# Moving the mLSTM scores, exponents and norms of a hybrid decoder layer in among its token projections

## The chip, the cores and the metric

The kernel runs on one core of one Trainium2 chip. The metric is the device time of one call in microseconds; the time before is the median of three runs. The engines are TensorE (PE, with PEld for its weight loads), VectorE (DVE), ScalarE (ACT), GpSimd (POOL) and SyncE (SP), which issues nearly all DMAs. Each engine works through its own list of instructions in order; the engines meet only at semaphores.

## The reference, cut to what matters

One decoder layer on 256 prompt tokens and 8 sequences of 4 sample tokens (288 columns in all), model width 1024: RMS norm, one input projection of 2824 columns, three mixers side by side, one output projection, and then a mixture of 32 experts (top 4 of 32, two matrices each), all in float32. The three mixers read disjoint columns of the projection: S5 (a diagonal complex recurrence, width 256, gelu, and a gated linear unit), RG-LRU (width 256), and mLSTM (4 heads of 128). The mLSTM part is what is changed most:

```python
mt = jnp.maximum(inter, jnp.max(dmat, axis=-1))
s = einsum('bhtd,bhsd->bhts', qc, kc) * exp(dmat - mt[..., None])     # decay matrix times scores
sc = exp(inter - mt)
num = einsum('bhts,bhsd->bhtd', s, vc) + sc[..., None] * einsum('bhtk,bhkv->bhtv', qc, cm)
den = sum(s, axis=-1) + sc * einsum('bhtk,bhk->bht', qc, nv)
h = num / maximum(abs(den), exp(-mt))[..., None]
c_new = decay[..., None, None] * cm + einsum('bhs,bhsk,bhsv->bhkv', ws, kc, vc)
h = h * rsqrt(mean(h * h) + EPS) * norm_g;   y = h * sigmoid(o)
```

The experts' weights are 32 x 12 MB, 403 MB in all; everything else that is read is about 23 MB.

## The kernel before, in words

The program is one block with one hand-ordered list for each engine. Its stages:

1. **Norm and input projection (0 to about 138 us).** x is normalised and turned into `hT` (channels x tokens). The projection's weights come in six chunks w_in0 to w_in5 through three slots of a ring. PE makes `channels` (a weight block stationary, 288 tokens moving, 16 matmul records each) for u, xr, gr, q and k, and `tokens` (tokens stationary, 256 weight columns moving) for v and o (`va`, `vb`, `oa`, `ob`, and `v2`, `o2` for the sample tokens).
2. **Gates and S5, in the same stretch.** DVE makes the mLSTM gate rows (`gsm`: a logarithm by a polynomial of eight steps, then scans), and says `m_rows` and `gate_rows`. ACT takes the exponentials of those rows and goes on to copy q2, q3, k0, k1 out of PSUM, in that order. POOL builds the S5 rotation table. Then S5 runs in eight pieces j: PE `s5_in(j)` fills two banks `bu{j}r` and `bu{j}i`, DVE `s5_scan(j)` rotates and scans them, POOL turns the result back (`s5_turned`), PE `s5_out(j)` adds it into `ys0` or `ys1`. RG-LRU work stands on DVE between the scans.
3. **mLSTM (about 138 to 190 us).** After the last token projection: gate rows turned (`rows`), the row maxima spread (`mb{h}`), scores (`st{h}`), on DVE the exponents' arguments and two multiplications, k turned (`kt`), memory products (`cp`), numerators (`nu`), on DVE the denominators and norms, on POOL k times its weights, v times its weights, and the decay of the state `c0` (L658).
4. **S5 gelu and gate.** DVE L1299 and L1300, then PE `glu`, ACT sigmoid, DVE `rg_used`.
5. **Output projection, residual, second norm, router (194 to 244 us)**, with the new sample state `c0` made on DVE by adding `cu` (L1313) and written out.
6. **Experts (from 244 us).** 16 pairs of experts of 12 steps each, 192 steps of 2 MB. Eight slots (`step_slot`: six in the ring, two in `ring_b`). SP may load step i once step i - 8 is done on PE. The eight first steps are loaded during stages 3 to 5 as the ring's slots come free.

PSUM has eight banks of 512 columns. The function `_place` gives each named fill a bank by its position in a list, and a number on that bank; `await_bank` lets PE start fill n of a bank only when fill n - 1 has been drained:

```python
def _place(names, banks):
    for i, name in enumerate(names):
        b = banks[i % len(banks)]
        FILLS[name] = (b, _fills_of[b])
        _fills_of[b] += 1
```

## Time and profile before

| | us |
|---|---|
| median of 3 runs (lowest, highest) | 1187.11 (1184.13, 1191.29) |
| the profiled execution, its time | 1186.5 |
| its span (first to last instruction) | 1184.8 |
| PE busy | 1110.9 (94%) |
| DVE busy | 364.8 (31%) |
| ACT busy | 163.4 (14%) |
| POOL busy | 137.9 (12%) |
| DMA over the span | 430.14 MB, mean 363 GB/s |

Busy shares are means over stages with different limits; the stages are told apart below by time from the span's start. In a timeline row the first number is the start, the second the busy time, then engine, line, operation, out<-in, shape and count; what stands in brackets is the idle time before it and who ended it. Matmuls in float32 leave two records each.

### The profile page before, as it was taken

Reading aid. Unit: us, or ns where it says so; the run is one execution under the profiler, and the core shown is the slowest. Engines: PE = TensorE matmul, PEld = TensorE weight load, DVE = VectorE, ACT = ScalarE, POOL = GpSimd, SP = SyncE. Lnnn points to the kernel's source line nnn. Section 1 sums busy time; section 2 is a strip of 40 time slices with the busy share of each in tenths; the row PEclk is TensorE's granted clock in tenths of the full one; section 3 lists DMA queues with packets and bytes.
Section 4 is the critical chain, followed back from the end, with each engine's and each line's share of the span. In section 5 each row is a group of like instructions: output and inputs, shape, how many; then the busy total and the mean of one; then the engine's idle time right before and its main releaser. Section 6 shows DMA issues by size and latency. Waiting matters only on the chain.

```text
span 1184.8 us, 12935 instructions
## 1 busy us (share of the span) xinstructions
PE 1110.9 (94%) x5051; PEld 463.6 (39%) x5051; DVE 364.8 (31%) x693; ACT 163.4 (14%) x304; POOL 137.9 (12%) x249
## 2 busy tenths in 40 slices
PE   6999767999999999999999999999999999999985
PEld 5766553443343334333433343333333332333221
DVE  5999985332121212121212122211312130203022
ACT  3312142211011001010101020101000100010002
POOL 7848753000000000000000000000000000000000
PEclk9989977999999999999999999999999999999998
DMA  8422343869999999999999999999999999999993
GB/s 228 157 92 71 130 177 142 320 266 392 427 426 422 427 428 426 427 429 428 426 429 429 427 428 429 428 426 429 429 427 428 429 428 427 429 429 426 428 428 150
DMA packets 79174, 430.14 MB, mean 363 GB/s; under 512 B 10730, under 2 KB 21202, under 8 KB 30242
## 3 DMA queue, kind: packets, MB, share of 16 engines
q1 hardware_dynamic: 78708, 428.47, 87.3%
q0 software_dynamic: 384, 1.18, 0.4%
q8 instruction: 22, 0.36, 0.1%
q14 instruction: 14, 0.11, 0.0%
q10 hardware_dynamic: 46, 0.01, 0.0%
HBM read 425.98 MB, written 3.67 MB: 363 GB/s over the span
## 4 chain that ended last, share of the span: by engine, by line
PE 67%; DVE 15%; DMA 12%; SPq 3%; ACT 1%; issue 1%; DVEq 0%; ACTq 0%
PE psum L1959 32%; PE psum L1972 15%; PE psum L1924 9%; DMA ring_a<-in_exp_w_dram 6%; DMA ring_b<-in_exp_w_dram 6%; PE psum L1934 4%; SPq L368 2%; PE psum L1983 1%; PE psum L1814 1%; PE psum L1943 1%; PE psum L1556 1%; DVE ring_a L1155 1%; DVE gsm L976 1%; DVE ring_a L1151 1%; DVE rgb L1299 1%
## 5 line engine op out<-in xcount | busy, mean ns | idle before, releaser
L1959 PE MATMUL psum<-ring_a,xg 128*64 128x512 f32 x1536 | 343.4, 596 | 7.6 <-DMA ring_a<-in_exp_w_dram 7.6
L1959 PEld LDWEIGHTS psum<-ring_a,xg 128*64 128x64 f32 x1536 | 105.0, 137 | 227.9 <-issue 210.1
L1972 PE MATMUL psum<-ring_a,aT 128*64 128x512 f32 x768 | 173.2, 597 | 8.8 <-DMA ring_a<-in_exp_w_dram 6.1
L1428 DVE TENSOR_TENSOR x<-x,psum 128x512 f32<-128x512 f32 x64 | 44.0, 688 | 364.6 <-PE psum L1934 364.6
L1959 PE MATMUL psum<-ring_b,xg 128*64 128x512 f32 x512 | 114.8, 595 | 0.2 <-DMA ring_b<-in_exp_w_dram 0.2
L1459 DVE TENSOR_SCALAR acts<-psum 128x512 f32<-128x512 f32 x32 | 22.0, 688 | 286.3 <-PE psum L1959 286.3
L1924 PE MATMUL psum<-S,xn 128*128 128x256 f32 (+1 forms) x384 | 109.0, 412 | 0.5 <-DVE S L1416 0.5
L1972 PEld LDWEIGHTS psum<-ring_a,aT 128*64 128x64 f32 x768 | 52.6, 136 | 110.6 <-issue 97.4
L1924 PEld LDWEIGHTS psum<-S,xn 128*128 128x128 f32 (+1 forms) x384 | 62.1, 187 | 53.6 <-issue 49.3
L1959 PEld LDWEIGHTS psum<-ring_b,xg 128*64 128x64 f32 x512 | 35.3, 137 | 73.6 <-issue 69.6
L884 ACT ACTIVATE acts<-acts 128x512 f32<-128x512 f32 x32 | 20.0, 626 | 316.4 <-DVE acts L1459 316.4
L1934 PE MATMUL psum<-yb,sgt 128*128 128x512 f32 x128 | 63.2, 617 | 0.0
L1556 PE MATMUL psum<-hT,ring_a 128*128 128x288 f32 x224 | 60.6, 433 | 1.9 <-DVE hT L994 1.4
L1972 PE MATMUL psum<-ring_b,aT 128*64 128x512 f32 x256 | 56.3, 592 | 1.4 <-DMA ring_b<-in_exp_w_dram 1.4
L877 ACT ACTIVATE xg<-psum 128x512 f32<-128x512 f32 x32 | 19.1, 598 | 276.7 <-PE psum L1924 276.7
L1556 PEld LDWEIGHTS psum<-hT,ring_a 128*128 128x128 f32 x224 | 45.4, 205 | 16.2 <-issue 3.2
L1432 DVE TENSOR_TENSOR x<-x,psum 32x256 f32<-32x256 f32 x64 | 26.5, 415 | 53.9 <-PE psum L1937 52.4
L1934 PEld LDWEIGHTS psum<-yb,sgt 128*128 128x128 f32 x128 | 21.8, 189 | 40.9 <-issue 40.9
L1972 PEld LDWEIGHTS psum<-ring_b,aT 128*64 128x64 f32 x256 | 18.7, 137 | 37.8 <-issue 37.3
L1565 PE MATMUL psum<-ring_a,hT 128*128 128x256 f32 x128 | 29.2, 384 | 2.1 <-DVE t_dve L1150 1.9
L1814 PE MATMUL psum<-ring_a,hT 128*128 128x512 f32 x64 | 30.5, 629 | 0.4 <-PE psum L1825 0.4
L909 ACT ACTIVATE yb<-psum 128x512 f32<-128x512 f32 x16 | 9.6, 597 | 140.2 <-PE psum L1972 140.2
(434 smaller groups left out, 825.8 us busy)
## 6 DMA issues: line engine op xcount, KB each, us to landing
ring_a<-in_exp_w_dram SPq DMA_DIRECT2D x144, 2048.0 KB, 25.9
ring_b<-in_exp_w_dram SPq DMA_DIRECT2D x47, 2048.0 KB, 27.4
ring_a<-in_w_in_dram SPq DMA_DIRECT2D x5, 2048.0 KB, 8.8
ring_a<-in_w_out_dram SPq DMA_DIRECT2D x2, 2048.0 KB, 10.1
ring_a<-in_state_ml_c_dram SPq DMA_DIRECT2D x4, 512.0 KB, 7.4
out_dram<-ring_a SPq DMA_DIRECT2D x4, 512.0 KB, 5.1
ring_b<-in_exp_w_dram SPq DMA_DIRECT2D x2, 1024.0 KB, 28.7
xn<-in_x_prompt_dram SPq DMA_DIRECT2D x2, 512.0 KB, 4.6
```

The costliest lines, as they stand in the source:

```text
L368: sp.dma_start(place, src).then_inc(slot_filled(il)[0], 16)
L884: A(sg1[:, x, :], gact[:, x, :], ACT.Sigmoid, scale=1.702).then_inc(sem("sig_ready"), 1)
L1428: TT(dst, dst, psum[0:n, banks[c], :], ALU.add).then_inc(sem("combine_added"), 1)
L1432: TT(dst, dst, psum[n * w:n * w + n, banks[c], 0:256], ALU.add).then_inc(sem("combine_added"), 1)
L1459: TSC(gact[:, x, :], psum[:, x, :], 7.0, None, ALU.min).then_inc(sem("g_clipped"), 1)
L1556: m = M(bank(name)[:, 0:T], w[:, k, col:col + 128], hT[:, k, :], start=(k == 0), stop=(k == KD - 1))
L1565: m = M(bank(name)[:, 0:256], hT[:, k, t0:t0 + n], w[:, k, col:col + 256], start=(k == 0), stop=(k == KD - 1))
L1814: m = M(bank(name)[0:n, :], hT[:, k, t0:t0 + n], slot_view(2 + c, 512)[:, k, :], start=(k == 0), stop=(k == KD - 1))
L1924: m = M(psum[:, 6 + c // 2 % 2, 256 * (c % 2):256 * (c % 2) + 256], xn[0:n, i, 128 * c:128 * c + 128], S[0:n, :, i].rearrange("p u x s -> ...
L1934: m = M(psum[0:n, bk, :], sgt[:, t0:t0 + n], yb[:, nn, :], start=True, stop=True)
L1959: m = M(psum[64 * x:64 * x + 64, bk, :], xg[:, k, u, 64 * x:64 * x + 64], w[:, 2048 * x + 512 * bk:2048 * x + 512 * bk + 512], start=False ...
L1972: m = M(psum[64 * x:64 * x + 64, 4 + nn, :], aT[:, 2 * j + s, 64 * x:64 * x + 64], w[:, 2048 * x + 1024 * s + 512 * nn:2048 * x + 1024 * s ...
```

## The change

- **Banks.** q and k get the banks 2, 3, 4, 5, 4, 5; the S5 fills `bu` have banks 0 to 3 to themselves; what follows from k2 on goes round 4, 5 and 7, and the numerators, o, `cp` and `nu2` round 4 and 5.
- **PE order.** `rows`, scores and numerators stand among the token projections; `nu2` before `ob1`; two small matmuls for every `mb` add a large constant (`far`, through `ident_bf`) where the mask is zero. The decay rows `dec` and `sc` share the bank of `rows`.
- **Exponents.** ACT takes them from PSUM, with the row's value as bias, into `E`; the clamp at 0 and the multiplication by the mask go. ACT also copies the scores to `stS`, and DVE multiplies `E` by `stS`, both in SBUF.
- **POOL to ACT.** k times its weights (eight ACT copies of 128x128 with a scale) and v times its weights (eight of 128x129). POOL's decay of `c0` goes: DVE does decay and addition in one operation for each head and sequence (32 of 128x129 for 12 of 128x387 or 128x258).
- **Norms.** ACT squares and copies each numerator to `nuS`; DVE makes all nine denominators at once, ahead of `s5_scan(7)`.
- **S5 gelu** in two halves (`s5_value(0)` after `s5_scan(5)`), the factor 0.5 moved into the sigmoid's scale and the last product.
- **Experts' biases**: loaded by ACT's queue in 128 rows, split in three pieces by ACT and DVE at about 22 to 41 us, and moved by 12 small DMAs from SP, for POOL's DMAs and its six-step rounding with ACT.
- **DMA order**: w_out before the first expert step, step 7 after the x reload.

```diff
-       "r0", "r1", "i0", "i1", "q0", "q1", "q2", "q3", "k0", "k1", "bu0r", "bu0i", "bu1r", "bu1i",
-       "k2", "k3", "bu2r", "bu2i", "va0", "va1", "bu3r", "bu3i", "vb0", "vb1", "bu4r", "bu4i",
...
-       "mb3", "st3", "kt0", "kt1", "kt2", "dec", "sc"], range(6))
+       "r0", "r1", "i0", "i1"], range(6))
+_place(["q0", "q1", "q2", "q3", "k0", "k1"], (2, 3, 4, 5, 4, 5))
+_place([f"bu{j}{x}" for j in range(J5) for x in "ri"], range(4))
+_place(["ys0"], (6,))
+_place(["k2", "k3", "rows", "mb0", "st0", "mb1", "st1", "va0", "mb2", "st2", "mb3", "st3", "smp", "va1", "v2", "vb0", "vb1",
+        "kt0", "kt1", "kt2"], (4, 5, 7))
+_place(["nu00", "nu01", "nu10", "nu11", "oa0", "cp0", "cp1", "oa1", "rgT", "ob0", "nu2", "ob1", "o2"], (4, 5))
...
             for h in range(2):
                 copy_out(f"q{h}", qT[:, h, :], bank(f"q{h}")[:, 0:T])
-            bias_round(0, 0)
 
             act.wait_ge(*at("gate_rows", 1))
...
+            def probabilities(h):
+                await_fill(act, f"mb{h}")
+                A(E[:, h, 0:256], bank(f"mb{h}")[:, 0:256], ACT.Exp, scale=-1.0, bias=rtok[:, 0, h:h + 1]).then_inc(sem("act_self"), 1)
+                A(E[:, h, 256:384], bank(f"mb{h}")[:, 256:384], ACT.Exp, scale=-1.0, bias=rtok[:, 1, h:h + 1]).then_inc(
+                    drained[FILLS[f"mb{h}"][0]], 1)
+                copy_out(f"st{h}", stS[:, h, :], bank(f"st{h}")[:, 0:384])
...
+            def e_prob(h):
+                b, f = FILLS[f"st{h}"]
+                dve.wait_ge(drained[b], f + 1)
+                says(TT(E[:, h, :], stS[:, h, :], E[:, h, :], ALU.mult), "e_ready", h + 1)
+
+            e_prob(0)
+            e_prob(1)
             s5_scan(3)
...
             s5_scan(5)
...
+            s5_value(0)
             s5_scan(6)
+
+            den, rv, sq = rsm[:, 48:57], rsm[:, 32:41], rsm[:, 16:25]
+            b, f = FILLS["nu2"]
+            dve.wait_ge(drained[b], f + 1)
+            dv(STT(out=den, in0=nuS[:, :, 128], scalar=-1.0, in1=nuS[:, :, 128], op0=ALU.mult, op1=ALU.max))
...
             s5_scan(7)
...
-                    drains(TT(c0[:, h, b0:b1, :], c0[:, h, b0:b1, :],
-                              bank(name)[:, 0:(b1 - b0) * 129].rearrange("p (b v) -> p b v", v=129), ALU.add), name)
+                    for n in range(b0, b1):
+                        ins_ = STT(out=c0[:, h, n, :], in0=c0[:, h, n, :], scalar=dec[:, h, n:n + 1],
+                                   in1=bank(name)[:, 129 * (n - b0):129 * (n - b0) + 129], op0=ALU.mult, op1=ALU.add)
...
+            scores(0)
+            scores(1)
+            s5_in(3)
+            tokens("va0", 3, 256, 0)
+            s5_out(0)
+            scores(2)
+            scores(3)
+            sample_scores()
+            s5_in(4)
+            tokens("va1", 3, 256, 1)
...
+            pe.wait_ge(*at("e_ready", H))
+            for i in range(2):
+                for hh in range(2):
+                    numerators(i, hh)
+            tokens("oa0", 4, 256, 0)
+            s5_out(4)
+            s5_in(7)
...
+            tokens("ob0", 5, 0, 0)
...
+            ends_fill(m, "nu2")
...
+            tokens("ob1", 5, 0, 1)
+            sample_tokens("o2", ((4, 256), (5, 0)))
...
+            s5_out(6)
```

## Rows read from the trace of the kernel before

**Rows 1.** Page, part 2: GB/s of all DMA in 40 slices of 29.6 us

```profile
GB/s 228 157 92 71 130 177 142 320 266 392 427 426 422 427 428 426 427 429 428 426 429 429 427 428 429 428 426 429 429 427 428 429 428 427 429 429 426 428 428 150
```

**Rows 2.** Chain that ended last: start, us, what

```profile
1128.55 31.78 DMA ring_b<-in_exp_w_dram
```

**Rows 3.** Timeline of SP: first load that waits for a finished expert step

```profile
255.29 24.43 SPq L368 DMA_DIRECT2D ring_a<-in_exp_w_dram  x6
```

**Rows 4.** Timeline of ACT around the gate rows

```profile
74.30 0.44 ACT L737 ACTIVATE xn<-gsm 4x288 f32<-4x288 f32 x1 [14.99 <-DVE gsm L1113]
...
75.37 0.68 ACT L670 ACTIVATE qT<-psum 128x288 f32<-128x288 f32 x2
75.95 0.67 ACT L670 ACTIVATE kT<-psum 128x288 f32<-128x288 f32 x2
78.39 0.68 ACT L745 ACTIVATE rgb<-rgb 128x576 f32<-128x576 f32 x1 [1.76 <-DVE rgb L1130]
```

**Rows 5.** Timeline of PE

```profile
56.64 15.76 PE L1556 MATMUL psum<-hT,ring_a 128*128 128x288 f32 x64 [0.45 <-PE psum L1556]
...
78.02 9.95 PE L1556 MATMUL psum<-hT,ring_a 128*128 128x288 f32 x32
87.90 1.23 PE L1590 MATMUL psum<-uT,ring_a 32*128 32x288 f32 x4
89.06 7.17 PE L1565 MATMUL psum<-ring_a,hT 128*128 128x256 f32 x32
...
97.33 0.67 PE L1597 MATMUL psum<-ring_a,wC 128*32 128x288 f32 x2
...
107.77 1.95 PE L1575 MATMUL psum<-ring_a,hT 128*32 128x128 f32 x64
...
185.43 4.21 PE L1795 MATMUL psum<-rgb,glw 128*128 128x288 f32 x8 [12.43 <-DVE rgb L1300]
...
193.94 3.67 PE L1814 MATMUL psum<-ring_a,hT 128*128 128x512 f32 x8 [0.41 <-PE psum L1825]
...
209.65 0.27 PE L1851 MATMUL psum<-ident,nbuf 128*36 128x128 f32 x1
```

**Rows 6.** Windows: us, then PE, PEld, DVE, ACT, POOL busy, PE clock, DMA

```profile
140.00:160.00 20.00, 14.29 (x72) 9.39 (x72) 17.72 (x31) 6.72 (x13) 14.12 (x19) 0.74 0.65 250
160.00:180.00 20.00, 9.22 (x118) 8.44 (x118) 15.80 (x37) 7.65 (x26) 10.97 (x11) 0.77 0.61 227
```

**Rows 7.** Timeline of DVE in the S5 scans and the mLSTM scores

```profile
79.97 0.46 DVE L1146 TENSOR_TENSOR ring_a<-psum,tabc 128x288 f32<-128x288 f32 x1
...
85.31 0.46 DVE L1146 TENSOR_TENSOR ring_a<-psum,tabc 128x288 f32<-128x288 f32 x1
...
129.80 0.46 DVE L1146 TENSOR_TENSOR ring_a<-psum,tabc 128x288 f32<-128x288 f32 x1
...
137.05 0.46 DVE L1146 TENSOR_TENSOR ring_a<-psum,tabc 128x288 f32<-128x288 f32 x1
...
144.29 0.76 DVE L1193 SCALAR_TENSOR_TENSOR hT<-rgb 128x576 f32<-128x576 f32 x1
...
156.01 0.56 DVE L1215 TENSOR_TENSOR ring_a<-ring_a,causal 128x384 f32<-128x384 f32 x1 [0.16 <-DVE ring_a L1210]
```

**Rows 8.** Timeline of POOL: an operation of the S5 turn, the decay

```profile
149.26 0.99 POOL L627 TENSOR_TENSOR ring_a<-ring_a,t_pool 128x288 f32<-128x288 f32 x1
...
177.04 8.02 POOL L658 TENSOR_TENSOR ring_a<-ring_a,dec 128x1032 f32<-128x1032 f32 x4
```

**Rows 9.** Timeline of DVE from the mLSTM outputs on

```profile
173.06 3.06 DVE L1290 SCALAR_TENSOR_TENSOR x<-psum,rsm,x 128x128 f32<-128x128 f32 x8
176.15 7.13 DVE L1299 SCALAR_TENSOR_TENSOR rgb<-rgb 128x576 f32<-128x576 f32 x1
...
191.35 2.33 DVE L1313 TENSOR_TENSOR ring_a<-ring_a,psum 128x387 f32<-128x387 f32 x4 [0.32 <-PE psum L1805]
...
216.95 0.14 DVE L1322 MEMSET lg<- 128x96 f32 x1 [10.58 <-DMA out_dram<-xn]
```

More of the change, by code:

```diff
@@ new lines, in _ @@
+            s5_out(5)
+            pe.wait_ge(sem("w_in5"), 16)
+            tokens("ob0", 5, 0, 0)
+            pe.wait_ge(sem("c0_loaded"), 64)
+            pe.wait_ge(*at("n_old", 1))
+            b, f = FILLS["v2"]
+            pe.wait_ge(drained[b], f + 1)
+            pe.wait_ge(*at("e_ready", H + 1))
+            await_bank(pe, "nu2")
+            for h in range(H):
+                r = slice(TS * h, TS * h + TS)
+                M(bank("nu2")[r, 0:129], E2[r, :], v2[r, :], start=True, stop=False)
```

717 lines of the change are left out of this document (312 added, 405 removed), and 4 rows, old and new, of tables (SAID, b).

## The prediction, made before the change was run

> **What bounds the kernel now.** I read the page's slices first. From the eleventh slice (296 us) on, the DMA engines move 422 to 429 GB/s in every slice but the last [rows 1]: the stream of expert weights is full, and the change touches nothing in it. The chain of waits agrees: near the end it stands on the landing of a weight load [rows 2]. So the last 900 us are a block of fixed length, and what counts is when it begins. It begins when PE has finished the first expert step and SP may load step 8, at 255.29 [rows 3]. Whatever moves this instant moves the end by the same amount, and the change is worth what it takes off the first 255 us.
>
> There I read the timelines of the engines one beside the other. Before 80 us DVE sets the pace. From 80 to 145 us DVE does eight scans with RG-LRU work between, and PE makes the token projections beside it. From 145 to 190 us the mLSTM goes through DVE, ACT, PE and POOL in turns: PE is busy 14.29 and 9.22 us of 20, at a clock of 0.74 and 0.77 [rows 6]. This is the stretch that the change empties. At 176.15 stands one multiplication of 7.13 us, of a shape that takes 0.76 elsewhere [rows 7, 9]; beside it POOL decays `c0` [rows 8].
>
> **Start of the change: a wait that it adds.** PE ran q2, q3, k0 and k1 from 56.64 to 72.4 without a wait [rows 5], because k0 and k1 had banks of their own. Now k0 has bank 4, which q2 holds. ACT drains q2 only behind the gate rows: it waits for DVE until 74.30, and copies q2 from 75.37 [rows 4]. So k0, which could start at 64.5, starts at about 75.8. DVE has two additional subtractions of 128x768 ahead of the gate rows; one falls in idle time, the other I take at 0.5 us net (bounds 0 and 2, as such an operation would take about 1 us by the 0.76 of 576 columns [rows 7], and other DVE work there runs with or without POOL). That gives 76.3.
>
> PE will have been idle for 11.8 us. After 12.43 us of idleness eight records took 4.21 us, 0.526 each, against 0.246 (15.76 for 64) [rows 5]; the 9.95 against 7.9 us of the 32 records from 78.02 says that the lower clock, 1.2 GHz, lasts about 6 us after PE resumes. Then k0 and k1 need 6.0 + 5.1 us, and k1 ends at 87.4. Behind the copy of k1 stands ACT's gate tanh (78.39 [rows 4]), and DVE's next operation waits for it. 87.4 + 0.5 for the copy + 0.7 for tanh + 0.8 for DVE's product: `s5_scan(0)` starts at 89.45, not at 79.97 [rows 7]. **The change loses 9.5 us here.**
>
> **The middle: PE against DVE.** PE's list from 87.4 to the end of `nu2`, durations from start to start [rows 5]: eight s5_in of 1.16 (9.3); k2 and k3 (7.9); seven token halves of 3.56 (24.9); `v2` 2.0; six s5_out of 1.09, two overlapping groups of 0.67 each (6.5). The small groups (rows, scores, turned k, numerators, `cp`, turned rg, `nu2`) are PE's busy time of 140 to 180 us, 23.5, and 1.5 before 140, less two s5_out: 22.8 at a clock of about 0.75 [rows 6], so 17.3 at the full clock; the far matmuls add 1.2. To this come 1.8 of waiting in the ping-pong of two banks (each numerator needs about 1.05 us of ACT: two squares and a copy) and 1.6 for `e_ready`. Sum 72.5: `nu2` ends at 159.9.
>
> DVE's list from 89.45: scan 5.34 when POOL is idle (79.97 to 85.31), 7.25 when POOL turns beside it (129.80 to 137.05) [rows 7]. Scans 0 to 6 make 48.2 with small variations; the RG-LRU work between, with one small copy less than before, 8.6; four score products from SBUF at 0.56 [rows 7] to 1.0, taken 0.85, E2 0.25; `wsm` and `qm` 0.8; `s5_value(0)` 2.2. With 0.7 waiting for ACT's square root, which now stands behind `va1`, DVE is through `s5_scan(6)` at 153.6. It then needs `nu2` drained for the denominators: 159.9 + 0.7 = 160.6. **A stall of 7 us on DVE**, ahead of `s5_scan(7)`. It costs less than it shows: denominators 1.6, and scan 7 now runs with POOL idle, 5.34, so it ends at 167.5. Before, it ended at 144.25.
>
> A rule of the Trainium skill speaks against the score products and output products that now take both inputs from SBUF. First the row: 7.13 us against 0.76 for the same shape, while POOL ran [rows 7 to 9]. The page SBUF — State Buffer, section Who interferes with whom, says that a DVE instruction with two SBUF inputs and a GpSimd instruction that reads SBUF exclude each other for a whole instruction. By it each of the thirteen products beside a turn may wait for one POOL operation, 0.99 [rows 8], so up to 13 us on DVE; by my sum 1.2 us. Of the 13, nine are in the next part, where the end of POOL's turn is awaited anyway, and the other four end before `nu2`, so that the sum stays.
>
> **Costed at nothing.** The twelve small bias DMAs leave SP while it waits for PE's first two channels of w_in1, with w_in4 behind them, which PE wants only some 70 us later; ACT's three bias copies of 768 columns (about 0.8 each) lie in its idle time before the gate rows (14.99 us of it at 74.30 [rows 4]). Uncovered they would cost about 2.5. The loads of `c0` leave 12 us later than before, at 122, with `v2`, but `nu2` wants them at 157; only if they were 25 us late would they count. ACT's k and v weights, 16 copies of about 0.2 to 0.3, stand where ACT waits for PE's fills.
>
> **The tail.** POOL turns scan 7 in six operations of at most 0.99 [rows 8], 5.9: 173.4. s5_out(7) on a PE that idled 7 us: 2.3, at 1.2 GHz. `s5_value(1)` 1.9, tanh 0.5, the second gelu product 0.5: 178.8. Meanwhile the nine output products (0.38 each [rows 9], 3.5, or 7 if POOL interferes) are done, as are the turned outputs, which hold PE till 180.4. The glu matmuls then run in 2.0 instead of 4.21, and the output projection starts at 182.4, against 193.94 [rows 5]: 11.5 earlier. This contains the 9.3 us that L1299 and L1300 lose no more.
>
> Of that the memory update takes back a part. DVE now makes 32 additions with decay at 0.38 (as a product of 128x128 [rows 9]), 12.2 us, where 12 additions took about 6.4 (four of 387 columns in 2.33 [rows 9], and smaller ones). The second group of `cu` must wait until the first is drained, at 188.4, while PE gets there at 186.9; the third group does not wait. PE ends the 16 output matmuls at 200.3 (before 209.65 [rows 5]), and the last part of `c0` is ready at 197.3. The stores, norms and DVE's restart (216.95 [rows 9]) follow one or the other as before, whence 9.1 to 9.3 earlier. DMAs fit in: some 12 MB between 176 us and these stores at 427 GB/s [rows 1] take 29 us, to 205, and the stores land at about 207.7. Bounds for queueing there: 0 and 3 us.
>
> **Sum.** -9.3 us at the instant of the first step, and at the end. The profiled execution took 1186.5 (span 1184.8); that makes 1177.2, and with the 0.6 us by which the median is above it, 1177.8, rounded to 1178. Own range of this case: gate rows +0 to +1.5, lower clock 4 to 8 us (-1 to +1), products +0 to +3, DMA +0 to +3, the denominators' stall -2 to +2: 1173 to 1187, mostly below 1184.
>
> **Rivals.**
>
> *The bank wait costs nothing in the end* (0.13). For it: what is delayed is PE, which had waits before. Against: tanh stands behind k1 on ACT, and DVE behind tanh. Were the 9.5 us not lost, or recovered by slack in the middle, the whole sum moves: 1178 - 9 = 1169.
>
> *PE becomes the bound of the middle more than I reckon* (0.19). Every group alternates on banks 4 and 5 or 4, 5 and 7, with ACT between, each turn 0.3 to 0.5 us. From k2 to `nu2` there are some 28 such fills; 0.2 us more on each makes 5.6 us. The time would be 1183.5; up to 1187.
>
> *PE stays at the lower clock* (0.08), which is the case that ends slower. Around 140 to 180 us, with small matmuls and gaps, the granted clock was 0.74 and 0.77 [rows 6]; now small matmuls stand all along the middle. Each microsecond of PE work at 1.2 GHz costs as much again. The gain is gone when 9 more of the 70 us of work run at 1.2 GHz, and the result is slower by over 0.5% from 15 on; with 20, the time is 1198. Against it: from 56.64 to 72.4 and from 87.9 on PE worked through without a gap and at the full rate, and the new list has hardly a gap. The Trainium skill, page TensorE: Matmul & The Clock Gate, part 1, says that the clock is low by default and activity releases it; by it the dense new list would keep the full clock.
>
> *The change does nothing that can be measured* (0.03): the middle is masked wholly by something that I do not see; 1187.
>
> **How the numbers follow.** The measurement tells differences over about 0.5%, 5.9 us: faster is under 1181.2. My own case has 0.57, of which 0.48 lies below 1181.2. With 0.12 of the first rival and 0.04 of the second: faster 0.64. Same: 0.09 + 0.13 + 0.03 and what is left of the others, 0.26. Slower 0.10: 0.08 and 0.02 of the second. The range 1168 to 1187 holds my case, the first rival and most of the second; outside stay the clock and the far ends.
>
> **What would show it.** Right: PE idle for about 11 us ahead of k0, released by ACT's copy of q2; `s5_scan(0)` at 88 to 91; DVE idle 4 to 9 us ahead of the denominators, released by ACT or PE of `nu2`; a short idle time of PE at the second group of `cu`; the first expert step loaded in the running loop at about 246; the GB/s of the slices after it as before. Wrong: no wait at k0; scan 7 done before `nu2`; a clock under 0.9 between 90 and 160; x1 or the stores landing later than DVE and PE want them; or a difference of the end that is not that of the first step.

## The result, and the profile after

The changed kernel took 1188.72 us (median of 17 runs, 1185.31 to 1191.33), the kernel before 1184.19 (17 runs, 1182.22 to 1192.49): ratio 1.0035, 95% interval 1.0022 to 1.0047. The forecast was 1178, with a range of 1168 to 1187, and so faster. The change makes the kernel slower by 0.35%, a small difference, but one that the interval tells from none. Its profiled execution took 1187.27 us with a span of 1185.5.

From the slices of the page (GB/s of all DMA, 29.6 us each):

```profile
GB/s 221 173 92 5 72 82 359 296 261 392 428 427 422 428 426 427 428 427 429 428 428 427 428 428 428 428 427 429 428 428 428 428 428 428 428 427 428 427 427 154
```

The stream is as full as before [rows 1], so the end is still the first expert step and a fixed rest. The timeline of PE, in the order of the steps of the prediction:

```profile
74.61 10.15 PE L1487 MATMUL psum<-hT,ring_a 128*128 128x288 f32 x32 [9.53 <-ACT qkT L629]
86.36 8.03 PE L1487 MATMUL psum<-hT,ring_a 128*128 128x288 f32 x32
...
103.95 2.28 PE L1521 MATMUL psum<-uT,ring_a 32*128 32x288 f32 x4
106.17 5.43 PE L1496 MATMUL psum<-ring_a,hT 128*128 128x256 f32 x16
...
118.58 3.72 PE L1496 MATMUL psum<-ring_a,hT 128*128 128x256 f32 x16
...
160.68 1.98 PE L1710 MATMUL psum<-ring_a 128*32 128x129 f32 x64
...
176.29 1.17 PE L1528 MATMUL psum<-ring_a,wC 128*32 128x288 f32 x2 [6.37 <-POOL ring_a L617]
...
184.30 4.11 PE L1761 MATMUL psum<-rgb,glw 128*128 128x288 f32 x8
188.24 3.60 PE L1735 MATMUL psum<-ring_a,hT 128*128 128x512 f32 x8
191.77 1.01 PE L1726 MATMUL psum<-ring_a 32*128 32x387 f32 x4
193.03 0.91 PE L1726 MATMUL psum<-ring_a 32*128 32x387 f32 x2 [0.24 <-DVE ring_a L1243]
...
207.94 0.27 PE L1788 MATMUL psum<-ident,nbuf 128*36 128x128 f32 x1
...
223.93 9.70 PE L1735 MATMUL psum<-ring_a,hT 128*128 128x512 f32 x16
...
252.66 10.52 PE L1898 MATMUL psum<-ring_a,xg 128*64 128x512 f32 x48
```

and of DVE:

```profile
85.89 0.76 DVE L1144 SCALAR_TENSOR_TENSOR rgb<-rgb 128x576 f32<-128x576 f32 x1 [8.72 <-ACT rgb L705]
...
124.82 1.05 DVE L1166 TENSOR_TENSOR rgb<-rgb 128x576 f32<-128x576 f32 x1 [7.74 <-ACT rgb L756]
...
163.68 0.18 DVE L1203 SCALAR_TENSOR_TENSOR rsm<-qkT 128x9 f32<-128x9 f32 x1 [9.64 <-ACT qkT L629]
...
172.94 4.99 DVE L1227 SCALAR_TENSOR_TENSOR x<-qkT,rsm,x 128x128 f32<-128x128 f32 x8
...
188.19 0.46 DVE L1236 SCALAR_TENSOR_TENSOR hT<-rgb 128x288 f32<-128x288 f32 x1 [5.54 <-ACT rgb L824]
...
189.54 9.20 DVE L1243 SCALAR_TENSOR_TENSOR ring_a<-ring_a,dec,psum 128x129 f32<-128x129 f32 x24
...
216.73 0.14 DVE L1253 MEMSET lg<- 128x96 f32 x1 [10.87 <-DMA out_dram<-xn]
```

The wait for bank 4 is there (9.53 us ahead of k0), and so is the stall ahead of the denominators (9.64). The output matmuls start at 188.24, 5.7 us earlier than before [rows 5], where 11.5 were forecast. From there on each mark gives some of it back: `nT` (the turned small norms, which are then stored) comes 1.7 us earlier, DVE's restart 0.2 earlier [rows 9], and SP's first running load 1.1 later than before [rows 3]:

```profile
256.36 24.43 SPq L370 DMA_DIRECT2D ring_a<-in_exp_w_dram  x6
```

The windows show PE's clock in the stretches where the time went (us, then PE, PEld, DVE, ACT, POOL busy, PE clock, DMA share, GB/s):

```profile
100.00:120.00 20.00, 20.00 (x78) 13.28 (x78) 16.11 (x29) 4.88 (x14) 11.06 (x14) 0.76 0.00 0
...
160.00:180.00 20.00, 12.78 (x168) 8.10 (x170) 14.50 (x34) 5.82 (x18) 5.47 (x7) 0.86 0.30 109
180.00:200.00 20.00, 19.52 (x52) 9.29 (x45) 10.68 (x29) 6.10 (x10) 0.00 (x0) 0.71 1.02 407
...
220.00:240.00 20.00, 17.28 (x87) 10.71 (x88) 10.29 (x27) 8.60 (x17) 0.00 (x0) 0.83 0.71 286
```

The first row is the one that nobody should pass over: PE is busy for all of its 20 us, and its clock is 0.76. A mean of 0.76 is a mixture of the two levels, 2.4 GHz (1.00) and 1.2 GHz (0.50). A stretch at the lower level is called a spell below.

### The profile page after: what moved, and what is told of

It reads as the page before. It is cut to its first block, busy times and chain, and to the rows that moved or that the text cites. A ratio compares the mean times of both kernels' runs of the same rounds, so it can differ in the third digit from the quotient of the medians.

```text
span 1185.5 us, 12954 instructions
## 1 busy us (share of the span) xinstructions
PE 1119.2 (94%) x5068; PEld 467.5 (39%) x5068; DVE 345.9 (29%) x683; ACT 166.0 (14%) x331; POOL 104.0 (9%) x204
## 3 DMA queue, kind: packets, MB, share of 16 engines
q1 hardware_dynamic: 79284, 429.06, 87.4%
## 4 chain that ended last, share of the span: by engine, by line
PE 74%; DMA 12%; DVE 7%; SPq 3%; issue 2%; ACT 1%; POOL 0%; DVEq 0%
PE psum L1898 31%; PE psum L1911 15%; PE psum L1861 9%; DMA ring_a<-in_exp_w_dram 8%; PE psum L1871 5%; DMA ring_b<-in_exp_w_dram 3%; PE psum L1487 3%; SPq L370 3%; PE psum L1496 2%; PE psum L1922 1%; PE psum L1882 1%; PE psum L1735 1%; DVE gsm L948 1%; PE psum L1521 1%; PE psum L1874 1%
## 5 line engine op out<-in xcount | busy, mean ns | idle before, releaser
L1911 PEld LDWEIGHTS psum<-ring_b,aT 128*64 128x64 f32 x256 | 18.7, 137 | 37.8 <-issue 37.3
L1735 PE MATMUL psum<-ring_a,hT 128*128 128x512 f32 x64 | 32.9, 670 | 0.0
## 6 DMA issues: line engine op xcount, KB each, us to landing
ring_a<-in_exp_w_dram SPq DMA_DIRECT2D x144, 2048.0 KB, 25.6
ring_b<-in_exp_w_dram SPq DMA_DIRECT2D x2, 1024.0 KB, 29.6
```

Of the source, the lines that this page charges most:

```text
L1735: m = M(bank(name)[0:n, :], hT[:, k, t0:t0 + n], slot_view(2 + c, 512)[:, k, :], start=first, stop=last)
L1911: m = M(psum[64 * x:64 * x + 64, 4 + nn, :], aT[:, 2 * j + s, 64 * x:64 * x + 64], w[:, 2048 * x + 1024 * s + 512 * nn:2048 * x + 1024 * s ...
```

## All runs on one page

Marks are starts in the profiled execution, in us: output matmuls, `nT`, DVE's restart, first expert step; then the span and what lies between the first step and its end. Ratios are to the kernel before, with the 95% interval. The kernel before was run beside each group of experiments and had medians of 1183.7 to 1184.4; the changed kernel was not, so that differences of medians to it are good to about 1 us.

| kernel | ratio | median | outputs | nT | restart | first step | span | rest |
|---|---|---|---|---|---|---|---|---|
| before | 1 | 1184.2 | 193.94 | 209.65 | 216.95 | 251.60 | 1184.8 | 933.2 |
| changed | 1.0035 (1.0022 to 1.0047) | 1188.7 | 188.24 | 207.94 | 216.73 | 252.66 | 1185.5 | 932.8 |
| b1_decay_folded | 0.9933 (0.9920 to 0.9946) | 1177.2 | 184.71 | 200.71 | 208.08 | 244.23 | 1176.8 | 932.6 |
| m1_decay_on_pool | 1.0025 (1.0007 to 1.0043) | 1187.3 | 194.16 | 209.94 | 218.70 | 254.67 | 1187.6 | 932.9 |
| e3_q_first | 0.9948 (0.9927 to 0.9969) | 1178.6 | 177.95 | 196.15 | 207.61 | 249.16 | 1183.6 | 934.4 |
| e4_den_late | 0.9994 (0.9981 to 1.0006) | 1181.7 | 181.59 | 201.36 | 210.27 | 246.54 | 1179.6 | 933.1 |
| e1_cu_early | 1.0015 (1.0000 to 1.0031) | 1185.4 | 188.51 | 204.45 | 214.81 | 250.15 | 1183.0 | 932.9 |
| e2_restart_free | 1.0031 (1.0017 to 1.0045) | 1187.1 | 188.19 | 207.89 | 216.40 | 252.47 | 1185.4 | 932.9 |
| e5_sqrt_first | 1.0025 (1.0009 to 1.0041) | 1188.1 | 187.32 | 205.52 | 217.53 | 253.94 | 1186.7 | 932.8 |
| e6_pe_filled | 1.0024 (1.0011 to 1.0038) | 1186.4 | 187.03 | 206.92 | 216.92 | 252.69 | 1185.8 | 933.1 |
| e12_apart_alone | 0.9996 (0.9981 to 1.0012) | 1183.5 | 184.09 | 202.16 | 211.05 | 246.93 | 1179.7 | 932.8 |
| e7_four_moves | 0.9912 (0.9898 to 0.9927) | 1173.8 | 171.61 | 188.26 | 199.96 | 235.01 | 1167.8 | 932.8 |
| e8_loads_late | 0.9870 (0.9834 to 0.9906) | 1169.6 | 170.80 | 187.41 | 196.02 | 237.35 | 1172.3 | 935.0 |
| e9_late_and_free | 0.9852 (0.9821 to 0.9883) | 1167.5 | 173.57 | 189.50 | 197.89 | 233.83 | 1166.7 | 932.9 |
| e10_scores_apart | 0.9850 (0.9821 to 0.9879) | 1167.4 | 169.52 | 185.94 | 197.88 | 239.31 | 1173.9 | 934.6 |
| e11_all_moves | 0.9827 (0.9814 to 0.9841) | 1162.8 | 168.91 | 184.84 | 193.20 | 229.51 | 1162.9 | 933.4 |

The last column is the first finding: over 16 kernels whose first step moves by 25 us, the rest is 932.6 to 933.4, and 934.4 to 935.0 in the three (e3, e8, e10) in which PE ran part of the first step itself at the lower clock (11.92 to 12.03 us for 10.52). The coupling of one to one, on which the whole forecast stands, holds.

## Experiments: one part of the change at a time

**The decay folded into the additions, in the kernel before.** What the forecast credited with 9.3 us is taken alone:

```
-            for h in range(H):
-                g.tensor_tensor(c0[:, h], c0[:, h], spread(dec[:, h, :].unsqueeze(2), 2, 129), ALU.mult)
...
-                    drains(TT(c0[:, h, b0:b1, :], c0[:, h, b0:b1, :], bank(name)..., ALU.add), name)
+                    for n in range(b0, b1):
+                        STT(out=c0[:, h, n, :], in0=c0[:, h, n, :], scalar=dec[:, h, n:n + 1], in1=bank(name)..., op0=ALU.mult, op1=ALU.add)
```

> The kernel before with one part of the change alone: GpSimd's four multiplications of the memory by its decay (8.02 us from 177.04) are gone and VectorE's 12 additions are 32 of one sequence each, with the decay as their scalar. Theory A (the port: VectorE's gelu product took 7.13 us and the halving 2.05 because GpSimd ran beside them, and the end moves with this chain): the two take 0.76 and 0.46 again, the gate's matmuls start near 177.5 instead of 185.43 us, outputs near 187 instead of 193.94; the additions cost 32 x 0.38 = 12.2 instead of 6.4 us, so nT moves by 2 to 5 us only: ratio 0.996 to 0.998. Rival B (as in the changed kernel, the additions of one sequence each give everything back): outputs start 7 us earlier and nT stands where it stood, ratio 1.000.

Ratio 0.9933, the first step 7.4 us earlier. DVE's timeline, to be held against [rows 9]:

```profile
174.40 1.52 DVE L1293 SCALAR_TENSOR_TENSOR rgb<-rgb 128x576 f32<-128x576 f32 x1
175.96 0.46 DVE L1294 TENSOR_SCALAR rgb<-rgb 128x576 f32<-128x576 f32 x1
...
182.05 4.58 DVE L1311 SCALAR_TENSOR_TENSOR ring_a<-ring_a,dec,psum 128x129 f32<-128x129 f32 x12
```

The product and the halving take 1.98 us instead of 9.18, with nothing changed but POOL's work beside them; the product still takes 1.52 and not 0.76, beside a multiplication of POOL's for the biases that ends at 175.30. (The Trainium skill, page SBUF — State Buffer, section Who interferes with whom, describes such an exclusive port between DVE and GpSimd; the rows of the product agree with it.) The 32 additions cost almost nothing more: an addition is 0.38 us, as forecast, but DVE begins the first twelve at 182.05, ahead of the output matmuls at 184.71, so that PE finds the banks free; outputs to `nT` is 16.0 us, before 15.7. So this one part wins 7 us, and all the rest of the change together loses 11.5 by the medians: 1188.7 against 1177.2.

**The same part undone in the changed kernel.**

```
+            for h in range(H):
+                g.tensor_tensor(c0[:, h], c0[:, h], spread(dec[:, h, :].unsqueeze(2), 2, 129), ALU.mult)
...
-                    for n in range(b0, b1): STT(... scalar=dec[:, h, n:n + 1] ...)
+                    dve.wait_ge(*at("c_decayed", h + 1))
+                    drains(TT(c0[:, h, b0:b1, :], c0[:, h, b0:b1, :], bank(name)..., ALU.add), name)
```

> The changed kernel with one part of the change undone: the memory's decay is again four multiplications on GpSimd (behind its last turn, near 176 us) and VectorE's additions are again 12 of two to three sequences. Theory A (the same part that gave the kernel before 7.2 us): GpSimd's 8 us from 176 lie over VectorE's S5 value and gelu products (178.6 to 182.6), one or two of which stretch to 7 us, the gate's matmuls start 6 us later; the additions end 4 us sooner after it; the first expert step 2 to 6 us later, ratio 1.006 to 1.008. Rival B (with the additions of one sequence each not hidden in the changed order, the old way is the cheaper): ratio 1.0035 or lower.

Rival B held: 1.0025, with an interval that overlaps the changed kernel's. The decays meet the output products, whose two large operands both stand in SBUF in the changed kernel (DVE, then POOL):

```profile
175.15 11.32 DVE L1232 SCALAR_TENSOR_TENSOR x<-qkT,rsm,x 128x128 f32<-128x128 f32 x8
```

```profile
178.67 7.65 POOL L623 TENSOR_TENSOR ring_a<-ring_a,dec 128x1032 f32<-128x1032 f32 x4
```

11.32 us instead of 4.99, and the outputs start at 194.16 instead of 188.24; but from there to `nT` it is 15.8 us instead of 19.7. The outputs lose 5.9 us, 2.2 of which were already lost at the last group of `nu2` (162.89 for 160.68, a spell that began later), and 3.9 come back behind them: the loss and the gain are of one size. The folding was worth 7 us in the kernel before, where its first additions come ahead of the outputs, and nothing that shows here; that the place of the additions makes the difference is argued, and no run shows it alone.

## Experiments: the waits

**k0's bank.** ScalarE copies q2 and q3 ahead of its wait for the gate rows:

```
+            for h in range(2, H):
+                copy_out(f"q{h}", qT[:, h, :], bank(f"q{h}")[:, 0:T])
             act.wait_ge(*at("gate_rows", 1))
...
-            for h in range(2, H):
-                copy_out(f"q{h}", qT[:, h, :], bank(f"q{h}")[:, 0:T])
```

> The changed kernel with ScalarE's copies of q2 and q3 put ahead of its wait for the gate rows, so that bank 4 is free for k0 as soon as q2 stands in it. By step (b) of the prediction: k0 starts near 66 instead of 74.61 us, k1 ends near 80, the first scan starts near 80 instead of 86.68, and TensorE's list moves 6 us with it: ratio near 0.998 if all of it reaches the end. Rival (later waits, for the numbers of VectorE's scans or for weights, give it back): the first scan moves by 6 us and the first expert step by under 1 us, ratio 1.003.

It beats its expectation: 0.9948, a median of 1178.6, 10.1 us under the changed kernel's. `nT` is 11.8 us earlier. The PE timeline:

```profile
73.99 9.69 PE L1487 MATMUL psum<-hT,ring_a 128*128 128x288 f32 x32 [1.00 <-ACT qkT L629]
...
169.20 1.17 PE L1528 MATMUL psum<-ring_a,wC 128*32 128x288 f32 x2 [6.39 <-POOL ring_a L617]
...
175.90 2.21 PE L1761 MATMUL psum<-rgb,glw 128*128 128x288 f32 x8
...
234.88 12.54 PE L1861 MATMUL psum<-S,xn 128*128 128x256 f32 x24 [0.51 <-DVE S L1347]
...
249.16 11.97 PE L1898 MATMUL psum<-ring_a,xg 128*64 128x512 f32 x48
```

The 32 records of k2 and k3 now start at 73.99, 12.4 us earlier, and the first scan at 78.07 instead of 86.68. The gate's matmuls ran at the full clock here, 2.21 us for 4.11, although the gap ahead of s5_out(7) is still there (6.39 us): the clock was low again when PE resumed, but came back after some 4.5 us, where the changed kernel's profile has 12. So what the tail costs after this gap differs between executions. The last two rows are why this profile's span gained only 1.9: the gather of 6.81 us took 12.54, and the first step 11.97 instead of 10.52. Its eight runs fall into two groups by granted clock: 1171.97 to 1176.57 at 0.981 or 0.982, and 1180.66 to 1185.50 at 0.973 to 0.975, four each. The theory of the expectation is right and its rival is wrong.

**The denominators behind scan 7.**

```
             s5_scan(6)
+            s5_scan(7)
...
             says(TSC(rv, rv, 1.0 / DK, EPS, ALU.mult, ALU.add), "nvar_ready", 1)
-            s5_scan(7)
```

> The changed kernel with VectorE's denominators moved from ahead of scan 7 to behind it, so that the scan runs in the 9.64 us in which VectorE waited for nu2. Theory A: scan 7 ends near 159.5 instead of 170.45 us, GpSimd's turn near 166, s5_out(7) waits no more (6.37 us), the products start when o2's gate is there, near 169.5 instead of 172.94, and TensorE, with no gap before it, runs the transposes and the gate's matmuls at the full clock (2 instead of 4.11 us): output matmuls start near 183 instead of 188.24, ratio near 0.999. Rival B: the output matmuls start earlier and the end doesn't move, ratio 1.0035. Rival C (the lower clock has another cause than that gap): the gate's matmuls still take 4.1 us and the start moves by only 2.5 us, ratio 1.0015.

The first step comes 6.1 us earlier; the median is 7.0 lower, and 4.9 by the ratios. DVE, then PE:

```profile
163.16 0.64 DVE L1204 SCALAR_TENSOR_TENSOR rsm<-qkT 128x9 f32<-128x9 f32 x1 [1.19 <-ACT qkT L629]
...
170.80 3.06 DVE L1227 SCALAR_TENSOR_TENSOR x<-qkT,rsm,x 128x128 f32<-128x128 f32 x8
```

```profile
168.25 0.69 PE L1528 MATMUL psum<-ring_a,wC 128*32 128x288 f32 x4 [0.34 <-PE psum L1506]
...
177.59 4.21 PE L1761 MATMUL psum<-rgb,glw 128*128 128x288 f32 x8
```

The stall of 9.64 us is 1.19, PE's of 6.37 ahead of s5_out(7) is gone, and theory A's amount came. Not all of its reason: the gate's matmuls still took 4.21, and PE now waited 3.00 us for the bank of the last turned output (`yT3`) shortly ahead of them. The eight output products take 3.06 us here, where POOL is through with its turn at 167.6, instead of 4.99. The prediction saw the stall and let it pass as cheap.

**The square root, ahead of va1's copy.**

```
+            A(rt[:], rt[:], ACT.Sqrt).then_inc(says_now("rg_root"), 1)
             v_out("va1", 1, 0)
-            A(rt[:], rt[:], ACT.Sqrt).then_inc(says_now("rg_root"), 1)
```

> The changed kernel with ScalarE's square root for the RG-LRU put ahead of its copy of va1 instead of behind it. VectorE waited 7.74 us for it up to 124.82 us. Theory A (that stall reaches the end, since GpSimd's last turn and the products hang on VectorE's list): the stall shrinks by 3 to 4 us and the first expert step comes as much earlier, ratio near 1.000. Rival B (between there and the products VectorE waits 9.64 us for nu2 anyway, and nu2 ends by TensorE's own list): scans 4 to 6 move earlier, the wait for nu2 grows by the same amount, the first expert step stays within 0.5 us, ratio 1.0035.

Rival B: DVE waits 4 us less for the root and 6 us more for `nu2`, which came 2.2 us later, as va1 ran at the lower clock (the last row, from PE; 3.72 in the changed kernel):

```profile
119.61 0.76 DVE L1166 TENSOR_TENSOR rgb<-rgb 128x576 f32<-128x576 f32 x1 [3.81 <-ACT rgb L755]
...
165.91 0.17 DVE L1203 SCALAR_TENSOR_TENSOR rsm<-qkT 128x9 f32<-128x9 f32 x1 [15.61 <-ACT qkT L629]
```

```profile
119.22 6.60 PE L1496 MATMUL psum<-ring_a,hT 128*128 128x256 f32 x16
```

A stall of 7.74 us, the largest in the middle that the prediction had missed (it gave 0.7), cost nothing that shows. As in e3, the gate's matmuls ran at the full clock behind an unfilled gap of 6.40 us (2.21).

**The first twelve additions ahead of the gate products.**

```
+            memory_added(0)
             for x in range(2):
                 says(STT(out=hT[:, x, :], in0=rt[:, x, :], scalar=0.5, in1=ri[:, x, :], ...), "rg_used", x + 1)
-            memory_added(0)
             memory_added(1)
             memory_added(2)
```

> The changed kernel with the first 12 of VectorE's 32 additions to the memory (group 0) moved from behind the S5 gate products to ahead of them, into the 5.54 us in which VectorE waits for the gate's sigmoid. Theory A (the end moves with VectorE's restart, and that restart follows from the last addition by way of nT and its store): 12 x 0.38 = 4.6 us of additions become free, the last one ends near 201.5 instead of 205.86 us, the restart comes near 212.5 instead of 216.73, the first expert step 4 us earlier, ratio to the kernel before near 1.000 instead of 1.0035. Rival B (the expert stream waits for its loads or for TensorE, not for this chain): the additions end earlier and the first expert step stays within 1 us of 252.66, ratio 1.0035.

```profile
182.94 4.58 DVE L1239 SCALAR_TENSOR_TENSOR ring_a<-ring_a,dec,psum 128x129 f32<-128x129 f32 x12
```

Outputs to `nT` falls from 19.7 to 15.9 us, but `nT` to the restart grows from 8.8 to 10.4: 2.5 us reach the first step, not 4. The mechanism is A's; what eats a part stands in the DMA queue (SP takes 8.21 us to issue the memory's four stores, for 4.26), and comes below.

**DVE's restart freed from the small stores.**

```
-            dve.wait_ge(sem("stored"), 16 * 10)
...
                     await_fill(dve, "wo2")
+                    dve.wait_ge(sem("stored"), 16 * 10)
```

> The changed kernel with VectorE's wait for the small stores moved from ahead of the residual additions to ahead of the sample rows' tile, the only one that shares memory with them. Theory A: the restart no longer waits for nT, its staging and its store (10.87 us of idle time end near 213 instead of 216.73), and the end gains what TensorE waits for VectorE there, 0.77 + 1.85 us: ratio near 1.001. Rival B (TensorE's own list from 207.94 us on sets the end, the restart being hidden): restart earlier, first expert step within 0.5 us of 252.66, ratio 1.0035.

A miss: the restart comes 0.3 us earlier, released by the landing of the router's bias instead of the `n` store. Both leave at the end of the same queue of SP. Taking away one of two releasers that come close together cures nothing.

## Experiments: the clock and the DMA queue

**The gap ahead of the gate filled.**

```
+            await_bank(pe, "yT1")
+            for _ in range(24):
+                M(bank("yT1"), ones_bf[:], spread(ones_bf[:].unsqueeze(1), 1, 4), start=True, stop=True)
             s5_out(7)
```

> The changed kernel with 24 bf16 matmuls of no use (5.6 us by the 0.234 us of the ones at 239.43) ahead of s5_out(7), in the 6.37 us in which TensorE waited for GpSimd; they go into a bank that is free. Theory A (the lower clock from 176 to 192 us follows from that gap): the gate's matmuls take 2.0 to 2.2 instead of 4.11 us, s5_out(7) 1.3 instead of 2.3, the output matmuls start near 185 instead of 188.24, and the first expert step is 3 us earlier, ratio 1.001. Rival C (the lower clock comes from another cause and stays): nothing moves, ratio 1.0035.

```profile
120.47 5.05 PE L1496 MATMUL psum<-ring_a,hT 128*128 128x256 f32 x16
...
173.03 5.35 PE L1741 MATMUL psum<-ones_bf 128*128 128x512 bf16 x24
...
184.98 2.21 PE L1764 MATMUL psum<-rgb,glw 128*128 128x288 f32 x8
```

Theory A holds for the fall: with the gap filled PE's clock stays at 1.00 up to the outputs, where it fell to 0.50 inside the unfilled gap in each of the seven other profiles that have it. From the start of `nu2`'s last group (163.88) to the outputs it is 23.15 us, against 27.56 in the changed kernel (160.68 to 188.24): 4.4 us less. But e3 and e5, with the gap unfilled and an early return of the clock, have 24.4 there, so that the fillers are worth between 1.2 and 4.4 us, by the length of the spell that would have followed. In this execution va1 at 120.47 met another spell, and `nu2` was 3.2 us late; 1.2 more went between `nT` and the restart. The medians are 2.3 us apart, the ratios 0.0011, and their intervals overlap: a gain in the runs is not shown.

**The scores apart.** What makes PE fall to its lower clock where it has no gap?

```
             scores(0)
+            tokens("va0", 3, 256, 0)
             scores(1)
             s5_in(3)
-            tokens("va0", 3, 256, 0)
             s5_out(0)
             scores(2)
+            tokens("va1", 3, 256, 1)
             scores(3)
```

> The changed kernel with va0 put between the scores of heads 0 and 1 and va1 between those of heads 2 and 3, on TensorE and ScalarE, and nothing else. Theory K (the scores' matmuls in a row bring TensorE to its lower clock): the spell from 100 to 112 us shrinks from 12 us to 7 or less, and the second one that two single moves showed behind the scores of heads 2 and 3 (3.2 us of nu2's time) doesn't come, so that the granted clock of the runs doesn't fall below 0.975 as in half of those of the changed kernel; ratio 1.000 where the changed kernel has 1.0035. Rival L: clocks from 0.971 to 0.978 as before and ratio 1.0035 to 1.006, since scan 3's numbers come 3.7 us later.

Windows of 4 us from 96 to 112, the changed kernel and then this one:

```profile
96.00:100.00 4.00, 4.00 (x34) 3.35 (x27) 3.79 (x7) 2.10 (x8) 2.48 (x4) 0.93 0.02 4
100.00:104.00 4.00, 4.00 (x13) 2.38 (x12) 3.76 (x8) 1.24 (x4) 3.69 (x5) 0.50 0.00 0
104.00:108.00 4.00, 4.00 (x9) 2.62 (x9) 3.76 (x8) 0.49 (x1) 1.67 (x3) 0.50 0.00 0
108.00:112.00 4.00, 4.00 (x15) 2.93 (x14) 3.76 (x8) 0.36 (x1) 0.00 (x0) 0.79 0.00 0
```

```profile
96.00:100.00 4.00, 4.00 (x35) 3.25 (x35) 3.76 (x8) 2.07 (x8) 2.40 (x5) 1.00 0.01 4
100.00:104.00 4.00, 4.00 (x14) 3.20 (x13) 3.79 (x7) 1.02 (x3) 3.70 (x4) 0.57 0.00 0
104.00:108.00 4.00, 4.00 (x20) 2.79 (x19) 3.76 (x8) 1.35 (x4) 2.21 (x3) 1.00 0.00 0
108.00:112.00 4.00, 4.00 (x19) 2.26 (x18) 3.79 (x7) 0.88 (x3) 1.71 (x3) 1.00 0.00 0
```

By the profile PE is busy for every microsecond of both. The spell shrinks from some 10 us to 3.5, and one of 3.4 us behind a wait of 0.69 at 140 us is not there either (nor is it in e4, so it may not be the edit that took it away); `nu2` starts its last group at 156.47 instead of 160.68, and the ratio is 0.9996, with an interval that lies below the changed kernel's: 5.2 us by the medians, 4.6 by the ratios. The eleven runs have granted clocks of 0.978 to 0.981, where the changed kernel's seventeen lie from 0.971 to 0.978. So the order of these matmuls decides how long the spell is, as theory K says. The changed kernel's runs differ with the clock as well: 1185.31 to 1187.01 in the three at 0.977 or 0.978, 1187.27 to 1190.70 in the seven at 0.975 (the profiled one is among them), 1188.54 to 1191.33 in the seven below. What about that block of scores brings the clock down is not shown, only that the spell is longer where they stand in one row. A second long spell on va1 stands in the profiles of e3, e5, e6 and e9, and in none of the three kernels with the scores apart.

**Four moves together**: q first, denominators late, first additions early, root first. No arithmetic is changed.

> The changed kernel with four moves together: q2 and q3 copied ahead of the wait for the gate rows, the denominators behind scan 7, the first 12 memory additions ahead of the S5 gate products, the RG-LRU's square root ahead of va1's copy. No arithmetic is changed. By the first steps of the single moves (selection ready 10.1, 6.1 and 2.5 us earlier; the square root unknown) and the fixed 933 us behind the first expert step: if they add up the first expert step comes near 234 us and the time near 1168.5, ratio 0.987. If the moves hide one another (the first and the second both shorten TensorE's wait ahead of the products), 1173 to 1176, ratio 0.991. Where TensorE falls to its lower clock ahead of the first expert step, as in the profile of the first move alone (the gather took 12.54 instead of 6.81 us), up to 8 us come on top.

0.9912: the first step of the profiled execution (1169.74 us, clock 0.983) comes 17.7 us earlier than in the changed kernel, of 18.7 by the sum of the three that counted (10.1, 6.1, 2.5). The other three runs took 1173.6 to 1174.17 (0.979 and 0.980), which is the case in which the moves hide one another; whether a spell or hiding took their 4 us is open, as the one profile is of the fastest run. Now `nT` to the restart is 11.7 us.

**The loads of steps 4 and 7 behind the `n` stores.**

```
-            load_step(0, 4)
...
-            load_step(0, 7)
...
             sp.dma_start(o[7][0, 0], stage[32:36, 0, :]).then_inc(sem("stored"), 16)
+            load_step(0, 4)
+            load_step(0, 7)
             load_step(0, 5)
```

> The four moves together, and the loads of expert steps 4 and 7 (2 MB each) put from ahead of the memory's stores to behind the n stores in SyncE's queue. Between nT and VectorE's restart 7.3 us lay in the kernel before, 8.8 in the changed one and 11.7 in the four moves, where the DMA engines were full from 160 to 210 us and SyncE needed 9.8 us to issue the memory's four stores. Theory D (that is a queue behind 4 MB of loads that came too early): the four stores are issued in 4 to 6 us, the restart comes 3 to 4 us sooner (near 196), ratio near 0.988. Rival E (the bytes have to be moved before the first steps anyway): the restart comes sooner and the expert steps wait for their loads near 231 us, ratio 0.991 as without the move.

SP's four stores of the memory, in the four moves and then with the loads late:

```profile
182.98 9.81 SPq L453 DMA_DIRECT2D out_dram<-ring_a  x4
```

```profile
182.20 4.05 SPq L450 DMA_DIRECT2D out_dram<-ring_a  x4
```

Theory D: issuing takes 4.05 us again, and the restart stands 8.6 us behind `nT` instead of 11.7. The medians are 4.2 us apart, but the runs of the two kernels (four and six) overlap. In the profile, as with e3, the gather ran at the lower clock (12.48 us), and the span hides it. Full DMA engines alone don't stretch the issue. In the changed kernel they were full from 180 us to the stores at 202.96 too, which took 4.26 us to issue; there the loads ran out as the stores began (287 GB/s from 204 on), while in the four moves the mean of the 10 us from 183 on is 348 GB/s.

**And DVE's wait moved**, by the edit of the restart above, on top of the late loads.

> As the run before, and VectorE's wait for the small stores ahead of the sample rows' tile alone. Alone in the changed kernel that gave 0.3 us, since the router's vectors landed only then. Theory D: with the DMA queue shorter the router's vectors land before the n stores do, the restart comes 1 to 2 us sooner again, ratio 0.987. Rival: the restart still waits for the router's bias, 0 us.

`nT` to the restart is 8.4 instead of 8.6 us, and it is the router's bias again that releases it: the rival. The median's 2.1 us less than e8's are within the spread of the six runs of each (1165.2 to 1175.7 and 1165.4 to 1170.7).

**The four moves and the scores apart**, without the late loads.

> The four moves together, with va0 put between the scores of heads 0 and 1 and va1 between those of heads 2 and 3 (on ScalarE too). In every kernel with the new order TensorE falls to its lower clock in a stretch in which it has no gap, always some 4 us into the block of the row transposes and scores, whose matmuls contract over 4 or 32 rows (100 to 112 us in the changed kernel, 88 to 104 in the four moves), and again behind the scores of heads 2 and 3 in two of them; in the kernel before it fell at 144 us, where its scores stood. Theory K (these matmuls, standing together, bring it down): with a token projection between them the stretch from 84 to 104 us stays at or near the full clock, TensorE's list is 4 to 5 us shorter up to nu2, ratio 0.988. Rival L (the fall has nothing to do with them): a spell of some 10 us stays between 84 and 110 us, and the time is 0 to 2 us longer since scan 3's numbers come 3.7 us later.

1167.4 against 1173.8, 6.4 us, though the profiled execution is again one with a slow gather. In windows of 4 us the spell between 84 and 104 us (five windows below the full clock) leaves two, 88 to 96.

**All seven moves.**

> The four moves, the two expert loads behind the n stores, VectorE's wait for the small stores ahead of the sample tile, and the scores apart: all seven moves, no arithmetic changed against the changed kernel. By 1167.5 us with the loads late and the wait moved, and 1167.4 with the scores apart, against 1173.8 without either: 6 us each, 1161.5 if they add up, ratio 0.981. If both only spared one of the spells at the lower clock that come and go from run to run, 1166, ratio 0.985.

1162.8 us, ratio 0.9827 (0.9814 to 0.9841), nearer to adding up than to hiding one another. It beats both kernels, by 21 and 26 us, with the arithmetic of the changed one. The scores' spell is not gone even here: 6.8 us from about 87 on, and 3.4 from 100 on.

## Why the prediction was wrong, point by point

The step that failed is the rate of PE. The sum charged the lower clock for the stretch behind the first wait and for s5_out(7) alone, and let PE run its list in the middle and the tail behind s5_out(7) at full speed. The profile of the changed kernel has 13.6 us at 1.2 GHz within that list and 12 from s5_out(7) on, worth 6.8 us and at least 3.2 over what was charged; the rest went behind the outputs, where the additions and the DMAs had been sized too small.

The sum said -9.3 us at the first step; the profiles say +1.06 (251.60 to 252.66). The 10.4 between them can be booked in full, to the rounding, in the prediction's own steps:

| step | forecast | measured | off by |
|---|---|---|---|
| k1 ends | 87.4 | 84.8 | -2.6 |
| PE's list, k1 to end of `nu2` | 72.5 | 77.9 | +5.4 |
| end of `nu2` to output matmuls | 22.5 | 25.6 | +3.1 |
| output matmuls to `nT` | 17.9 | 19.7 | +1.8 |
| `nT` to DVE's restart | 7.3 as before | 8.8 | +1.5 |
| restart to first step | 34.65 as before | 35.93 | +1.3 |

The table is of two executions. The medians are 4.5 us apart and the two profiled executions 0.8: the changed kernel's median lies 1.5 above its profile, and the kernel before's over 17 runs 2.3 below its own (and 2.9 below the median of three that the forecast started from).

*The wait at the start.* Mechanism right: released by q2's copy, 9.53 us, first scan at 86.68. Its price was not: k0 started at 74.61 and not at 76.3, k0 and k1 took 10.15 us and not 11.1, and the first scan came 6.7 us later than before, not 9.5. Taking the wait away gave 10.1 us by the medians of e3, more than it had cost at that place, as k2 now starts 4.0 us earlier than in the kernel before; that the two numbers are close is luck. The rival by which the wait costs nothing falls.

*PE's list in the middle.* The sum of the matmuls was right: with the scores apart `nu2` ended at 158.5, 73.1 us after k1's end at 85.3, where 72.5 was forecast; so the rival of 0.2 us more on each of 28 fills falls too. (That list still has a spell of 3.4 us in it.) What failed is the rate. The prediction took the full clock for a list without gaps, and named the other case its rival with 0.08 and a price of 1 us for each at 1.2 GHz. That rival is what happened, in small: 10.2 us at the lower clock in a stretch without a gap and 3.4 from 140 us on, 6.8 us lost, of which the list had 1.4 to spare. (Its own sign of being wrong, a clock under 0.9 between 90 and 160 us, is the window of 0.76.) A second spell on va1, seen in the profiles of e3, e5, e6 and e9, is the likely reason why the median lies another 1.5 us above the changed kernel's profiled execution; no profile of a slower run of it shows this. The rule of the Trainium skill that stood against it (page TensorE: Matmul & The Clock Gate, part 1) is that activity releases the throttle. The rows on the gap agree with it, as the clock fell there unless the 24 fillers stood in it; the windows from 100 to 108 us, with 4.00 us busy of 4.00 at 0.50, don't agree with it.

*The tail.* POOL's turn took 5.7 us, of 5.9 forecast, and s5_out(7) 2.1, of 2.3. The prediction charged the lower clock to s5_out(7) and not to what follows it: the transposes and the gate's matmuls ran at it up to 188, 4.11 us where 2.0 was said. This is the term of 3.1 us, and its size is that of one execution: in e3 and e5 the clock came back before the transposes, and the same stretch took 3.2 us less. e6 puts 1.2 to 4.4 us on that gap. The gap itself was avoidable: the stall ahead of the denominators, "It costs less than it shows", cost 6.1.

*The additions.* 0.38 us each was right, and so was the mechanism, PE waiting for the first group's banks. The size was off: the gate's products come last on DVE and began at 188.19, so the additions started behind PE's first outputs; 3.8 us by e1, where the forecast had about 2.2 (17.9 from the outputs to `nT`, for 15.7 before).

*DMA and the last rows.* The DMAs were to fit in, with bounds of 0 and 3 us and nothing in the sum: 1.5 us in the changed kernel, 4.4 in the four moves. The bytes did fit. In the changed kernel SP issues the `n` stores 1.4 us earlier than before, but from there to the restart it is 5.5 us instead of 4.3; in the four moves what waited was SP, whose issue of four stores stretches beside loads that are still moving. Of the last 1.3 us, 0.9 are the second half of the output matmuls, 9.70 us where they took 8.83 before, at a clock of 0.83 in that window.

*Costed at nothing, and free indeed*: the bias DMAs and copies, the later `c0`, ScalarE's weights, and ScalarE's root (7.74 us of stall, behind which DVE waits for `nu2` anyway). The SBUF operands decided nothing in the forecast's middle; the eight output products took 4.99 us beside POOL's turn, where the forecast had 3.5 for nine, and 3.06 without it.

*The gain itself.* The two gelu operations, credited with 9.3 us, gave 7.2 by b1. That part had 7 us to give, and the rest of the change lost 11.5.

## What to carry to other kernels

Split a large change before judging it: one part of this one was worth 0.7% alone, and the rest took back 1.0%; three waits in it, each removed by moving a few lines, cost more than that together (17.7 us at the first step). When a fixed stream stands behind a prologue, measure each edit at the marks ahead of the stream, and by the median of many runs; a slow gather hid 8 us in the spans of single executions here, and most of that in their first steps too. A stall that a forecast finds is a place to reorder, as two of them here were worth 10 and 6 us, and PE time is only known with a clock: look at the granted clock of every stretch, above all of those without a gap.

## What the runs showed of the hardware

- PE falls to 1.2 GHz in stretches in which it is never idle by the profile: for 10 us from 99.5 in the changed kernel, and from 88 to about 101 in the four moves. It does so again in some executions only: va1 took 3.72, 5.05, 6.58 or 6.60 us, the gather 6.81 or 12.54. Token projections between the scores shorten the first kind (to 3.5 us). What brings the gather's spell, which costs a run 7 to 8 us, is open.
- After the same wait of 6.4 us and with the same matmuls behind it, PE's clock came back after 4.5 us in two executions (e3, e5) and after 12 to 14 in four (the changed kernel, e1, e2, e12): the gate's matmuls took 2.21 in the first, 4.11 to 4.21 us in the others.
- POOL's multiplications held up DVE where both of DVE's large operands are in SBUF: 7.13 us for 0.76 in one place. The eight output products show all four cases: 3.06 us with an operand in PSUM beside a multiplication of POOL's (the kernel before, b1), 3.06 with both in SBUF and POOL idle (e4), 4.99 with both in SBUF beside POOL's turn, 11.32 beside its decays (m1). So an operand that moves from PSUM to SBUF costs nothing by itself, but opens a place for the collision.
- SP takes 4.05 us to issue four stores, 4.26 where full DMA engines have just run out of loads, and 9.81 where loads of 2 MB are still moving beside them.
